# The states' products ahead of the inverse's sums on TensorE in one kind of phase of an RWKV-7 recurrence

## The reference

```python
def step(S, inp):
    r_t, w_t, k_t, v_t, a_t, b_t = inp
    sa = jnp.einsum('bhij,bhj->bhi', S, a_t)
    S = S * w_t[:, :, None, :] + sa[..., None] * b_t[:, :, None, :] + v_t[..., None] * k_t[:, :, None, :]
    y = jnp.einsum('bhij,bhj->bhi', S, r_t)
    return S, y
```

## Time and profile before

| what | us |
|---|---|
| median of 3 executions | 2121.35 (2117.09 to 2128.88) |
| the profiled execution | 2109.07 |
| its span, first to last instruction | 2107.3 |
| PE busy in the span | 1948.6 (92%) |
| DVE busy | 1290.7 (61%) |
| ACT busy | 779.1 (37%) |
| rounds 1 to 7 (by the span's clock) | about 313 to 672 |

### The profile page before, as it was taken

One profiled execution on the slowest core, in us unless ns is written; L12 is line 12 of the kernel. 1 busy time (PEld: TensorE's weight loads), 2 busy tenths in 40 slices (PEclk: granted clock), 3 DMA queues, 4 the chain that ended last, 5 costly groups with the idle time before them and its releaser, 6 DMA issues.

```text
span 2107.3 us, 37544 instructions
## 1 busy us (share of the span) xinstructions
PE 1948.6 (92%) x15616; PEld 1837.5 (87%) x15616; DVE 1290.7 (61%) x2061; ACT 779.1 (37%) x1346; POOL 167.0 (8%) x167
## 2 busy tenths in 40 slices
PE   4999988888889998999999989988999899999996
PEld 4889867777777898999999989986679899999996
DVE  7655466888874568772366454165755976326754
ACT  6654254555554242221122133236754322112222
POOL 0000222222230000000000000003300000000000
PEclk9999988999999999999999999999999999999998
DMA  4112000000002212212221122416521121222111
GB/s 171 41 61 68 9 3 15 15 15 15 14 14 83 86 60 70 71 65 85 91 81 57 65 80 81 155 60 252 186 96 61 61 80 66 76 82 79 65 64 63
DMA packets 30328, 150.72 MB, mean 72 GB/s; under 512 B 4785, under 2 KB 7601, under 8 KB 17873
## 3 DMA queue, kind: packets, MB, share of 16 engines
q1 hardware_dynamic: 30160, 148.32, 20.2%
HBM read 137.84 MB, written 10.47 MB: 70 GB/s over the span
## 4 chain that ended last, share of the span: by engine, by line
PE 80%; DVE 12%; ACT 5%; issue 3%; DMA 0%; DVEq 0%; POOL 0%; ACTq 0%; SPq 0%; POOLq 0%
PE ps L642 18%; PE ps L644 18%; PE ps L643 18%; PE ps L1458 3%; PE ps L733 2%; PE ps L734 2%; PE ps L735 2%; DVE gram L1934 1%; DVE w_lo L637 1%; PE ps L2139 1%; PE ps L1443 1%; DVE mix_f L1222 1%; DVE x_lo L791 1%; PE ps L2159 1%; PE ps L1489 1%
## 5 line engine op out<-in xcount | busy, mean ns | idle before, releaser
L642 PE MATMUL ps<-x_hi,w_hi 128*128 128x320 f32 x2192 | 688.2, 314 | 58.0 <-DVE w_lo L637 27.5
L644 PE MATMUL ps<-x_hi,w_lo 128*128 128x320 f32 x2192 | 684.2, 312 | 0.0
L643 PE MATMUL ps<-x_lo,w_hi 128*128 128x320 f32 x2064 | 644.3, 312 | 0.0
L637 DVE TENSOR_TENSOR w_lo<-raw,w_hi 128x2048 fp32r<-128x2048 f32 (+3 forms) x109 | 227.3, 2086 | 403.1 <-ACT w_hi L631 403.1
L642 PEld LDWEIGHTS ps<-x_hi,w_hi 128*128 128x128 f32 x2192 | 419.3, 191 | 62.8 <-issue 32.5
L644 PEld LDWEIGHTS ps<-x_hi,w_lo 128*128 128x128 f32 x2192 | 418.9, 191 | 0.0
L643 PEld LDWEIGHTS ps<-x_lo,w_hi 128*128 128x128 f32 x2064 | 394.6, 191 | 0.2
L631 ACT ACTIVATE w_hi<-raw 128x2048 fp32r<-128x2048 f32 (+3 forms) x109 | 190.1, 1744 | 414.3 <-PE ps L644 414.3
L642 PE MATMUL ps<-hid_hi,w_hi 128*128 128x320 f32 x704 | 217.4, 309 | 0.0
L643 PE MATMUL ps<-hid_lo,w_hi 128*128 128x320 f32 x704 | 217.4, 309 | 0.0
L644 PE MATMUL ps<-hid_hi,w_lo 128*128 128x320 f32 x704 | 217.4, 309 | 0.0
(11 more groups left out here) (274 smaller groups left out, 2953.2 us busy)
## 6 DMA issues: line engine op xcount, KB each, us to landing
raw<-in_w_gate SPq DMA_DIRECT2D x22, 1024.0 KB, 4.8
raw<-in_w_up SPq DMA_DIRECT2D x22, 1024.0 KB, 4.8
raw<-in_w_down SPq DMA_DIRECT2D x16, 768.0 KB, 4.3
raw<-in_w_down SPq DMA_DIRECT2D x16, 640.0 KB, 3.8
raw<-in_w_kv SPq DMA_DIRECT2D x8, 1024.0 KB, 4.8
past_k<-in_past_k SPq DMA_DIRECT2D x8, 1024.0 KB, 6.9
past_v<-in_past_v SPq DMA_DIRECT2D x8, 1024.0 KB, 4.8
raw<-in_w_r SPq DMA_DIRECT2D x4, 1024.0 KB, 6.8
```

Source lines behind the costliest of these rows:

```text
L637: dve.tensor_tensor(w_lo[:, c % 2, 0:n], raw[:, c % 2, 0:n], w_hi[:, c % 2, 0:n].bitcast(F32), SUB) \
L642: pe.matmul(out, w, x, start=start, stop=False)
L643: pe.matmul(out, w, xl, start=False, stop=False)
L644: return pe.matmul(out, wl, x, start=False, stop=stop)
```

## The change

In `pe_rec`, phases now come in two kinds by another test: the states' products go first in every phase that is not "off".

```diff
     def pe_rec(pe, i):
         for k in range(SLOTS):
-            states_first = PHASES[k][0] == "inv"
+            states_first = PHASES[k][0] != "off"
             if tile_of(i - 1) and states_first:
                 pe_states(pe, i - 1, k)
             if tile_of(i):
                 pe_merge(pe, i, k)
...
             if tile_of(i - 1) and not states_first:
                 pe_states(pe, i - 1, k)
```

## The result

The change makes the kernel slower: 2147.57 us (2145.07 to 2150.0, four executions) against 2124.22 (2117.09 to 2128.88, four). The ratio on record is 1.0151 [1.0122, 1.0179], that is 1.5%. The quotient of these two medians is 1.011; with the medians of before in the later measurements (2114.70 to 2119.56) it is 1.013 to 1.016. I had forecast 2139 against 2121.35, a ratio of 1.0083. The direction is right, and the median lies in the range, near its top, but partly by luck: the waits cost less than I had summed, and the clock, for which the sum had no term, cost more.

The account below looks back on a forecast made before the run. PE (busy 45.7 of 51.2 us a round) and DVE (43.9) bound the kernel, each delaying the other. Rounds 2 to 6 at 2.9 us and rounds 1 and 7 at 1.8 gave +18.1 on 2121.35: 2139 us, range 2126 to 2152.

Parts of the forecast that it names:

- the sum: Whole kernel: 2.9 us in each of rounds 2 to 6, 1.8 each in rounds 1 and 7, together +18.1 us.
- The lag, 0.25: At all four places: 0.25 us from a DVE end to a PE start, read at k = 13's mask, used for `u_pre`.
- +1.91 for both: k = 4 and k = 7 together: "out" at k = 7 comes 1.91 us later, 0.54 of it from k = 4.
- The step that DVE becomes late: Behind k = 4: later sums delay DVE's additions, its idle 0.56 is used up, and the state comes 0.93 us later.
- the meeting of `state_d` and POOL: k = 7: `state_d` takes 1.07 us beside POOL's instruction, so `su_pre` binds; without that, k = 7 costs 0.29.
- 0.49 forecast: k = 10: 0.39 us from waiting for the copy plus 0.10 for one more change of tile, +0.49.
- The 0.49 of k = 13: k = 13: 0.39 us from the copy plus 0.10 for a change of tile; the 0.62 wait stays and grows.
- I see no slack that takes 2.9 back: From "out" of k = 14 on: state, `ra` and grams form a chain, so the round keeps its whole 2.9 us.
- taken back later: Rival, end of round: DVE's 1.28 us idle at k = 14 swallows part; +9 us, 2130 us, chance 0.15.
- the rival that the clock falls in more rounds: Rounds 2 to 6: more idle time brings low-clock stretches of 5.2 us each; 2145 to 2165 us, chance 0.14.
- the signs that I had set: Wrong if rounds keep their length, "u" does not wait for its copy, or PEclk falls below 1.00 in rounds 3 to 6.
- the new pieces are each under 0.8: Against the clock falling: round 4 held 1.00 despite 5.5 us idle, up to 1.3 at one place; new waits are shorter.

Follow-up runs that it names:

- e1_fill: The changed kernel with one 256-column matmul that nothing reads ahead of each "u" in the four add phases, rounds 1 to 6: 2136.92 us, ratio 1.0103.
- e8_wait_only: The kernel before, nothing moved, but at k = 4 of rounds 1 to 7 the sums wait for the copy to `u_pre`: 2133.6 us, ratio 1.0076.
- e9_wait_k3fill: The kernel before with the sums waiting for `u_pre` at k = 4, plus three matmuls that nothing reads at k = 3: 2123.81 us, ratio 1.0017.
- e2_k4: The kernel before with the states' products first at k = 4 only among the four changed places: 2135.79 us, ratio 1.0095.
- e5_after_k3fill: The changed kernel with three matmuls that nothing reads ahead of "pre" at k = 3 of rounds 1 to 6: 2143.5 us, ratio 1.0124.
- e6_before_k3fill: The kernel before with three matmuls that nothing reads at k = 3 of rounds 1 to 6: 2112.9 us, ratio 0.9975.
- e7_before_fill: The kernel before with unread matmuls: three at k = 3, three in rounds 0 to 6's first off phase, five before round 0's level 1 transposes: 2113.41 us, ratio 0.9986.
- e12_before_fill2: The kernel before with unread matmuls: three at k = 3 and five more ahead of round 0's transposes of level 2: 2111.25 us, ratio 0.9958.
- e3_k7_10_13: The kernel before with the states' products first at k = 7, 10 and 13, and k = 4 left as before: 2136.45 us, ratio 1.0100.
- e4_between: Against the kernel before, "u" placed between the sums of part 0 and those of part 1 at k = 4, 7, 10 and 13: 2129.34 us, ratio 1.0070.
- e10_k13_only: The kernel before with the states' products first at k = 13 only among the four changed places: 2132.21 us, ratio 1.0076.
- e11_k7_only: The kernel before with the states' products first at k = 7 only among the four changed places: 2130.12 us, ratio 1.0059.

## Why the prediction was wrong, and where it was right

**The direction, and the wait.** Right, by its own step: "u" waits for the copy, two instructions later in DVE's list than the mask, and the sums stand behind it. The forecast of 10 to 14 us of such waits came out at 10.1 and 0.2.

**The lag, 0.25.** Too long for this wait. After, the copy of round 5 ends at 556.39 (DVE's row below) and "u" starts at 556.54: 0.15. It is 0.15 at k = 10 and 13 of that round too (574.40 to 574.55, 581.90 to 582.05).

```profile
556.10 0.29 DVE L2018 COPY u_pre<-ps 128x128 f32<-128x128 f32 x1 [0.78 <-PE ps L1483]
```

**k = 4 and k = 7 at full clock.** Forecast +1.91 for both; e1_fill's round 4 has 0.95 + 0.81 = 1.76. The step that DVE becomes late and the state comes 0.93 later is the 0.95: in e1_fill DVE makes the state without the idle 0.56 of the earlier trace rows.

```profile
496.24 0.57 DVE L2030 SCALAR_TENSOR_TENSOR state_p<-ps,decays,state_d 64x64 f32<-64x64 f32 x2
```

At k = 7 the two cases that I gave can both be seen. With the meeting of `state_d` and POOL I had 1.91 from the start of the round, that is 0.98 behind the 0.93; without it 0.29. In e1_fill's round 4 they meet, and the stretch grows by 0.81:

```profile
498.13 1.54 POOL L1800 TENSOR_TENSOR tmp_q<-kk,gate_a 128x640 f32<-128x640 f32 x1 [0.92 <-DVE gate_a L1966]
...
498.69 1.06 DVE L2023 TENSOR_SCALAR state_d<-state_p,decays 128x128 f32<-128x128 f32 x1
```

After, in round 5, `state_d` starts when POOL is almost done, takes 0.28, and the stretch grows by 0.30:

```profile
565.16 1.54 POOL L1800 TENSOR_TENSOR tmp_q<-kk,gate_a 128x640 f32<-128x640 f32 x1 [3.00 <-DVE gate_a L1966]
...
566.64 0.28 DVE L2023 TENSOR_SCALAR state_d<-state_p,decays 128x128 f32<-128x128 f32 x1
```

**k = 10 and k = 13.** k = 10 was right (0.49 forecast, 0.40 and 0.44 measured; with 0.15 for the lag it would have been 0.39). The 0.49 of k = 13 failed at "I see no slack that takes 2.9 back". There was some, in how DVE and POOL meet between the wait and the next grams. Timelines of both, before:

```profile
552.67 2.18 POOL L1810 TENSOR_TENSOR bk<-k_t,e_neg 128x640 f32<-128x640 f32 x1 [11.01 <-issue]
554.81 1.68 POOL L1814 TENSOR_TENSOR ra<-r_t,c_mid 128x384 f32<-128x384 f32 x2
```

```profile
552.62 0.82 DVE L1975 TENSOR_TENSOR bk<-tmp_q,e_neg 128x640 f32<-128x640 f32 x1
...
555.97 1.21 DVE L1981 SCALAR_TENSOR_TENSOR ra<-kk,c_sum 128x640 f32<-128x640 f32 x1
```

After:

```profile
583.44 1.55 POOL L1810 TENSOR_TENSOR bk<-k_t,e_neg 128x640 f32<-128x640 f32 x1 [12.63 <-issue]
584.94 2.28 POOL L1814 TENSOR_TENSOR ra<-r_t,c_mid 128x384 f32<-128x384 f32 x2
```

```profile
584.15 1.52 DVE L1975 TENSOR_TENSOR bk<-tmp_q,e_neg 128x640 f32<-128x640 f32 x1
...
587.14 0.82 DVE L1981 SCALAR_TENSOR_TENSOR ra<-kk,c_sum 128x640 f32<-128x640 f32 x1
```

In these rows the instruction that starts second is the one that takes longer. Before, DVE's `bk` began 0.05 ahead of POOL's L1810 and took 0.82, and `ra` (L1981) began while POOL was in L1814 (to 556.49), and took 1.21. After, the later sums push `bk` behind the start of POOL's L1810 (to 584.99); `bk` takes 0.70 longer, but in time in which DVE used to wait for PE (0.93 ahead of the state), and `ra`, which starts when POOL's L1814 is almost done (587.22), takes 0.82. PE's first gram gets back the 0.39. So the waits cost 2.25 a round, not 2.9. I had given "taken back later" 0.15; of the four places it held for this one.

**The clock.** This is the step that failed: the sum has no term for it, and I gave the rival that the clock falls in more rounds 0.14. By the signs that I had set I was wrong: PEclk fell below 1.00 in rounds 3 to 6, and PE's busy time in round 5 did not stay, but grew by 3.5 us. My reason against it was that round 4 held 1.00 although PE idles for 5.5 of its 51.2 us, and that "the new pieces are each under 0.8". The size of the single piece was the wrong thing to look at: in e8_wait_only one of 0.38 us, 0.85 us of work behind the 1.3 that was there, brings down the clock in every one of rounds 2 to 6. With it, a place that costs 0.44 (e9_wait_k3fill) or 0.95 (e1_fill) at full clock costs 3.25 to 3.39 (e8_wait_only, e2_k4). Without it the waits would have cost 12.8 us, a ratio of 1.006, where I had summed 18.1. That is an estimate: five rounds of 2.25, and 1.5 for the outer two (round 7 grew by 0.66 at k = 4 and 0.21 at k = 7, round 1 by 0.22 at k = 7 and 0.39 at k = 10). The rest of the 36.3 us by which rounds 1 to 7 grew in the trace came with the clock. I had priced a low stretch at 5.2 us and one in each of five rounds at +26. The one at k = 4 of round 5 adds only 2.4 to its wait (3.34 against 0.95), but rounds 1, 4, 6 and 7 lost the clock at other places too.

The Trainium skill, TensorE: Matmul & The Clock Gate, section "A second HAM failure mode: psum-queue depth-cycling", has short, frequent idling between groups of matmuls make the clock swing between the two levels. The rows at 0.67 and 0.50 above agree with it, and I had weighed it too low.

**What stays open.** Over all traces, the clock was down at k = 4 in all 15 of the rounds 2 to 6 in which PE stands still both ahead of k = 4 (the 1.3 us) and in it (the change, e2_k4, e8_wait_only). It was down in 2 of 30 where fill-in products stand in one of the two places (e1_fill, e5_after_k3fill, e6_before_k3fill, e7_before_fill, e9_wait_k3fill, e12_before_fill2). With the 1.3 us alone it was down in none of 5 before, and in 11 of 20 where only a later place or the order was changed. Why some of the rounds 3 to 6 of e3_k7_10_13, e4_between, e10_k13_only and e11_k7_only fall at k = 4, where their order is that of before or nothing waits, and which of the rounds do, no run settles. That e9_wait_k3fill holds the clock in three of five rounds shows that PE's standing still ahead of the place matters; it doesn't show how. Its rounds 2 and 3 differ from 4 to 6 only in when they come; whether that decides, no run tests.

## What to carry to other kernels

Before a wait is put on TensorE, look at what it stands next to: one of 0.4 us, close behind an idle 1.3 that had done no harm in rounds 2 to 6, cost 3.3, because the clock fell. Compare PE's busy time for the same matmuls first: as much as it grew, slower matmuls cost, and not waits. And a product that waits for a copy goes behind ready work that covers the copy; the old order did that. Cover alone is not enough: e4_between has it too, with no new wait of PE, and is slower by 0.7%, so the clock is to be read again after every change of order.

## What was not expected of the hardware

- The price of a standstill is not local. With the wait at k = 13 alone (e10_k13_only) its own stretch grows by 2.5 and, in three rounds of five, the next k = 4 by 4.33.
- The slow instructions are not those that waited: in round 5 after the change "u" (from 556.54) and "s_from" ran at full clock, and the sums behind them (from 558.15) were slow, though PE had not stood still in between.
- Matmuls that compute nothing pay: three in each of rounds 1 to 6 and five in round 0 make the kernel before 0.42% faster by the medians (e12_before_fill2).
- The same kernel differs from one execution to the next with its mean clock: of 31 executions of before one at 0.975 took 2108.81 us, one at 0.964 took 2129.52, about 1.9 us for each 0.001.
